# Wide experts: rows kept by chunk and gathered whole in fp32, first pair alone; a ring of eleven places with three filled during the even layer

## The chip, the cores and the metric

One NeuronCore of a Trainium2 chip runs one launch of one kernel. The metric is the device time of that launch in microseconds. Everything is fp32 in memory: 256 tokens of width 1024 go through three layers, and 578 MB are read, nearly all of it weights.

## The reference

The input `x` is [1, 256, 1024]. Three layers follow each other, each a token mixer and a mixture of experts:

```python
x = first_block(x, ...)                     # GLA + gated delta mixer, then 32 narrow experts, rms_norm
for layer in range(2):                      # second_block
    mix = even_mixer(x, ...) if layer % 2 == 0 else fourier_mixer(x, w_out)
    x = layer_norm(ALPHA * x + mix, ln1_gain[layer], ln1_bias[layer])
    ffn = hierarchical_moe_2(x, ...)        # 32 wide experts
    x = layer_norm(ALPHA * x + ffn, ln2_gain[layer], ln2_bias[layer])

# hierarchical_moe_2: every token chooses two of the 32 experts
xs = xt[tok]                                                       # rows sorted by expert
hid = silu(ragged_dot(xs, w_gate, sizes)) * ragged_dot(xs, w_up, sizes)
ys = ragged_dot(hid, w_down, sizes) * gate                         # weighted by the router
out = segment_sum(ys, tok)                                         # back to the tokens
```

The first block's experts have the hidden width 256 (narrow: 1 MB for each of the three matrices), those of the two layers of the second block 512 (wide: 2 MB each). In every layer the weights of all 32 experts are read.

## The kernel before

**Expert stage.** `stage_packed` runs once for the narrow layer (tag `one`) and once for each wide layer (tags `l0`, `l1`; the profile leaves the number out and prints `l`). It treats the experts two at a time, 16 pairs `p`, each expert with 64 slots (`CAP`), so that a pair fills 128 partitions. For each pair TensorE does, in this order:

- the gate product `hidden(p, 0, G)` (L1718): gathered rows as 64-column weights, expert weights moving, 512 columns in a wide layer, 32 records;
- two transposes of the gated one-hot matrix (L1758) into `TP`;
- the up product `hidden(p, 1, Up)` (L1718);
- `scatter(p - 1, 0)` and `scatter(p - 1, 1)` (L1728, L1729): the previous pair's output, sent back to its tokens by a product with the one-hot matrix `oneT`;
- the transposes of the hidden rows (L1770), which wait for VectorE's product of the silu and the up half (L1861);
- `scatter(p - 1, 2)` and `scatter(p - 1, 3)`. The fourth shares a PSUM bank with the first and waits for its add;
- at the end of a batch of pairs `gather(b)` (L1705, L1706): the rows of the next batch, by a product with the one-hot matrix `one`, turned on the way. Its PSUM banks are the scatter's too, so it waits for all four adds of VectorE (L1835). A batch is two pairs in a wide layer, four in the narrow one. ScalarE copies the gathered blocks out (L1796), and the next pair starts when all of a batch are out;
- `down(p)` (L1741), which waits for ScalarE's copy of the turned hidden rows (L1804).

**Split rows.** Gather and scatter multiply by a matrix of zeros and ones. To keep fp32 values whole with the `fp32r` type, each value is held as a rounded high half and the rest as a low half, and each product is done twice, once with each: `h_high` and `h_low` for the rows (ScalarE L1452, GpSimd L1477, both in the route stage), `yh` and `yl` for the pair's output (ScalarE L1814, VectorE L1871).

**Weights.** SP loads the experts' weights in chunks of 2 MB (`Experts.load`, L1618), in the order in which they are used: a wide pair has six, a narrow one three. Each chunk goes to the next place of a ring; the transfer is issued when TensorE has used up the chunk that was there before (`s_used`). A wide layer has ten places: six in `pool`, two in `gate_room`, two in `store`. The even mixer uses `pool` and `store` itself, so the first chunks of layer `l0` are issued in its route stage.

**Route stage.** `stage_out_route` does the mixer's output product (L1397), residual, normalization (L1509, L1510 write `x`), turns the rows to `hT` (L1405), computes the router's logits and picks two experts per token on VectorE (L1514 to L1563). `stage_norm` is the normalization after the experts (L1314 to L1326); it loads its gain and bias rows itself. After layer `l0` it also has SP load the Fourier tables, `w_out_fourier` and two chunks of layer `l1`; `stage_fourier` adds four, and the route stage the rest. All of SP's transfers go in the order in which SP issues them.

The stages stand behind each other with a barrier between them, in the order in `build`: mixer, route `one`, experts `one`, `stage_norm_f`, even mixer, route `l0`, experts `l0`, norm, Fourier, route `l1`, experts `l1`, norm.

## Time and profile before

| what | value |
|---|---|
| median of 3 runs | 1990.39 us (1990.31 to 1991.92) |
| the profiled execution | 1990.57 us, span 1988.7 us |
| TensorE busy | 1770.2 us, 89% of the span, mean granted clock 0.951 |
| VectorE, ScalarE, GpSimd busy | 678.9, 426.0, 83.7 us |
| read from HBM | 577.65 MB, 292 GB/s over the span |
| first wide expert stage | 984 to 1436 us |
| second wide expert stage | 1521 to 1972 us |
| a wide chunk, median from issue to landing | 28.0 to 32.6 us |

The span runs from the first to the last instruction of the profiled execution; 1.9 us of the time lie around it. In the trace a TensorE row "128\*64" is a product with 64 weight columns; two such can run at the same time, so that their mean duration is longer than their distance. A record is one instruction of the trace. The busy column of a group divided by its count is its distance when the products follow each other closely. A wait is the idle time of an engine ahead of an instruction, with the one that released it behind the arrow.

### The profile page before, as it was taken

Reading aid. Unit: us, or ns where it says so; the run is one execution under the profiler, and the core shown is the slowest. Engines: PE = TensorE matmul, PEld = TensorE weight load, DVE = VectorE, ACT = ScalarE, POOL = GpSimd, SP = SyncE. Lnnn points to the kernel's source line nnn. Section 1 sums busy time; section 2 is a strip of 40 time slices with the busy share of each in tenths; the row PEclk is TensorE's granted clock in tenths of the full one; section 3 lists DMA queues with packets and bytes.
Section 4 is the critical chain, followed back from the end, with each engine's and each line's share of the span. In section 5 each row is a group of like instructions: output and inputs, shape, how many; then the busy total and the mean of one; then the engine's idle time right before and its main releaser. Section 6 shows DMA issues by size and latency. Waiting matters only on the chain. (4 is left out here: it accounts for less than half of the span.)

```text
span 1988.7 us, 20708 instructions
## 1 busy us (share of the span) xinstructions
PE 1770.2 (89%) x8544; PEld 949.7 (48%) x8544; DVE 678.9 (34%) x1371; ACT 426.0 (21%) x705; POOL 83.7 (4%) x66
## 2 busy tenths in 40 slices
PE   7999897895789999799799999998777999998895
PEld 6884454695455555456434433333244344433331
DVE  3658242446223333543412221221333122222223
ACT  2421224452222221222211111111112111111110
POOL 0000001311100000120100000000001000000000
PEclk9999998797889999899799999999987999999998
DMA  5345230004659997341999999999795999999995
GB/s 196 128 151 176 104 122 4 0 1 188 251 237 398 403 422 283 132 170 42 408 400 423 423 423 423 424 423 423 297 382 230 424 423 423 423 423 423 423 423 225
DMA packets 100017, 581.75 MB, mean 293 GB/s; under 512 B 23947, under 2 KB 26251, under 8 KB 34893
## 3 DMA queue, kind: packets, MB, share of 16 engines
...
HBM read 577.65 MB, written 2.62 MB: 292 GB/s over the span
## 5 line engine op out<-in xcount | busy, mean ns | idle before, releaser
L1718 PE MATMUL up_ps_l<-pool,hT 128*64 128x512 f32 x640 | 143.3, 596 | 12.6 <-DMA pool<-in_expert_w_up 12.6
L1718 PE MATMUL gate_ps_l<-pool,hT 128*64 128x512 f32 x640 | 141.4, 593 | 6.6 <-DMA pool<-in_expert_w_gate 5.3
L447 PE MATMUL proj_ps<-pool,hT 128*128 128x512 f32 x320 | 141.4, 602 | 5.6 <-DVE pool L685 5.6
L1741 PE MATMUL y_ps_l<-pool,hidden_l 128*64 128x512 f32 x640 | 142.4, 596 | 2.4 <-ACT hidden_l L1804 1.4
L1871 DVE SCALAR_TENSOR_TENSOR y_low_l<-y_ps_l,slot_gate_l,y_high_l 128x512 fp32r<-128x512 f32 x64 | 47.1, 751 | 251.0 <-ACT y_high_l L1814 251.0
L439 PE MATMUL proj_ps<-hT,pool 128*128 128x256 f32 x512 | 111.9, 380 | 0.0
L1861 DVE TENSOR_TENSOR hidden_l<-hidden_l,up_ps_l 128x512 f32<-128x512 f32 x32 | 22.0, 688 | 246.8 <-PE up_ps_l L1718 246.8
L439 PEld LDWEIGHTS proj_ps<-hT,pool 128*128 128x128 f32 x512 | 96.9, 190 | 14.8 <-issue 1.8
L447 PEld LDWEIGHTS proj_ps<-pool,hT 128*128 128x128 f32 x320 | 61.8, 194 | 82.1 <-issue 75.4
L1718 PEld LDWEIGHTS gate_ps_l<-pool,hT 128*64 128x64 f32 x640 | 45.4, 137 | 98.5 <-issue 87.7
L1718 PEld LDWEIGHTS up_ps_l<-pool,hT 128*64 128x64 f32 x640 | 43.7, 137 | 98.3 <-issue 77.9
L1814 ACT ACTIVATE y_high_l<-y_ps_l,slot_gate_l 128x512 fp32r<-128x512 f32 x64 | 44.0, 688 | 203.0 <-PE y_ps_l L1741 199.5
L1741 PEld LDWEIGHTS y_ps_l<-pool,hidden_l 128*64 128x64 f32 x640 | 43.9, 137 | 88.0 <-issue 77.6
L1705 PE MATMUL gather_ps_l<-onehot_l,h_high_l 128*128 128x256 f32 x256 | 68.0, 302 | 16.9 <-DVE x L1835 12.8
L1801 ACT ACTIVATE hidden_l<-gate_ps_l 128x512 f32<-128x512 f32 x32 | 34.3, 1073 | 214.8 <-PE gate_ps_l L1718 214.8
L1804 ACT ACTIVATE hidden_l<-gate_ps_l 128x512 f32<-128x512 f32 x32 | 19.2, 599 | 278.6 <-PE gate_ps_l L1770 278.6
L1706 PE MATMUL gather_ps_l<-onehot_l,h_low_l 128*128 128x256 f32 x256 | 66.0, 295 | 0.0
L1835 DVE SCALAR_TENSOR_TENSOR x<-x,gather_ps_l 128x512 f32<-128x512 f32 x96 | 62.9, 683 | 1.6 <-PE gather_ps_l L1729 1.6
L1705 PEld LDWEIGHTS gather_ps_l<-onehot_l,h_high_l 128*128 128x128 f32 x256 | 52.0, 203 | 23.1 <-DVE x L1835 18.9
L1397 PE MATMUL out_ps_l<-store,hT 128*128 128x512 f32 x128 | 55.7, 593 | 2.4 <-PEq L2455 1.3
L1796 ACT ACTIVATE hT<-gather_ps_l 128x512 f32<-128x512 f32 x64 | 38.3, 598 | 67.0 <-PE gather_ps_l L1706 67.0
L1706 PEld LDWEIGHTS gather_ps_l<-onehot_l,h_low_l 128*128 128x128 f32 x256 | 52.2, 204 | 0.0
...
## 6 DMA issues: line engine op xcount, KB each, us to landing
...
```

The lines of the kernel that those rows point to most:

```text
L439: last = mm(pp[:, n % 2, m * T:(m + 1) * T], wbuf[n % 2][:, c, m * P:(m + 1) * P], k.hT[:, c, :], start=(c == 0), stop=(c == KC - 1))
L447: last = mm(pp[:, n % 2, j * W:(j + 1) * W], k.hT[:, c, j * P:(j + 1) * P], wbuf[n % 2][:, c, :], start=(c == 0), stop=(c == KC - 1))
L1397: last = nc.tensor.matmul(y[:, j, n, :], k.hT[:, c, j * P:(j + 1) * P], w_out[:, c, n * W:(n + 1) * W], start=(c == 0), stop=(c == KC - 1))
L1705: mm(at, k.h_high[:, j, c], moving, start=(j == 0), stop=False)
L1706: last = mm(at, k.h_low[:, j, c], moving, start=False, stop=(j == NJ - 1))
L1718: last = mm(out[e * CAP:(e + 1) * CAP, 0:H], xg(part * r + c)[:, at:at + CAP], ex.weights(i, e, c), start=(part + c == 0), stop=(part == e ...
L1741: last = mm(Y[e * CAP:(e + 1) * CAP, n], hidT[:, part * r + c, e * CAP:(e + 1) * CAP], ex.weights(i, e, c)[:, n * W:(n + 1) * W], start=(p ...
L1796: nc.scalar.activation(to, got, ACT.Copy).then_inc(s_xg, 1)
L1801: nc.scalar.activation(hid[:].rearrange("p (c n) -> p n c", c=HT), G[:, 0:H].rearrange("p (n c) -> p n c", c=HT), ACT.Silu).then_inc(s_sg, 1)
L1814: nc.scalar.activation(yh[:, n], Y[:, n], ACT.Copy, scale=slot_gate[:, 0:1]).then_inc(s_yh, 1)
L1835: nc.vector.scalar_tensor_tensor(out=xs, in0=xs, scalar=1.0 if p else alpha, in1=scatter_bank[o], op0=ALU.mult, op1=ALU.add).then_inc(s_ad ...
L1871: nc.vector.scalar_tensor_tensor(out=yl[:, n], in0=Y[:, n], scalar=slot_gate[:, 0:1], in1=yh[:, n].bitcast(F32), op0=ALU.mult, op1=ALU.sub ...
```

## The change

- The wide layers no longer split rows. The second `stt` of the normalization writes the rows by chunk into a new tile `k.h` (fp32), from which the gather and the transposes to `hT` read; ScalarE's `high` and GpSimd's subtraction stay for the narrow layer alone. The gather is one fp32 product where it was two of fp32r, and so is the scatter; `yl` and its two VectorE operations are gone there. The first pair's adds read the old rows from `k.h`.
- The batches of a wide layer are pair 0 alone, seven of two pairs, and pair 15 alone.
- Order in all three layers: the first scatter (in the last pair of a batch the first two) goes ahead of the up product, the fourth has the bank `Up` and goes behind the transposes of the hidden rows; the first two blocks of a gather go ahead of these transposes, the others behind. The gate product waits for the gathered blocks one by one.
- The ring of the wide layers has eleven places; the new one is `first_room`. Three chunks of layer `l0` are issued at the end of the even mixer's loads (`early`), six and two in its route stage; three instead of two of layer `l1` in the norm stage ahead of the Fourier mixer.
- The norm rows of `stage_norm` are loaded in the route stage (`k.ln2_rows`).
- Tiles of the even mixer and the narrow layer move into `gate_room`; `stage_norm_t` becomes `stage_turn`, with what was not used left out; the scratch that the compiler keeps in SBUF for GpSimd's transfers goes down to 1024 bytes a partition. Code that only runs when an expert has more than 64 tokens follows suit.

```diff
                     else:
                         o(stt(out=xj, in0=xj, scalar=mv[:, j, 0:1], in1=g[:], op0=ALU.subtract, op1=ALU.mult))
-                        stt(out=xj, in0=xj, scalar=rs[:, j, 0:1], in1=b_row[:],
-                            op0=ALU.mult, op1=ALU.add).then_inc(s_h, 1)
+                        by_row = "p (i c) -> p i c"
+                        stt(out=k.h[:, j].rearrange("p c i -> p i c"), in0=xj.rearrange(by_row, c=KC), scalar=rs[:, j, 0:1],
+                            in1=b_row[:].rearrange(by_row, c=KC), op0=ALU.mult, op1=ALU.add).then_inc(s_h, 1)
...
-    def __init__(self, k, before, tag, H, batch, w_gate, w_up, w_down):
-        self.tag, self.H, self.HT, self.batch, self.dram = tag, H, H // P, batch, (w_gate, w_up, w_down)
+    def __init__(self, k, before, tag, H, batch, split, w_gate, w_up, w_down):
+        self.tag, self.H, self.HT, self.split, self.dram = tag, H, H // P, split, (w_gate, w_up, w_down)
+        first = batch if split else 1
+        self.batches = [list(range(first))] + [
+            list(range(p, min(p + batch, NE // 2))) for p in range(first, NE // 2, batch)]
...
-        scatter_bank = [XG[:, 0], XG[:, 1], SC[:], XG[:, 0]]
...
-        def xg(c):
-            return xg_first[:, c] if c < here else xg_rest[:, c - here]
...
+
...
+
+            return 2 if new_batch(p) else 1
+
         def new_batch(p):
-            return p % GB == GB - 1 and p < NI - 1
+
+            b, _ = ex.batch_of[p]
+            return b + 1 if p == ex.batches[b][-1] and p < NI - 1 else 0
...
-                def gather(b):
-
-                    pe.wait_ge(s_pm, b + 1)
-                    for n in range(KC // PER):
+                def gather(b, first, end):
+
+                    width = len(ex.batches[b]) * P
+                    if first == 0:
+                        pe.wait_ge(s_pm, b + 1)
+                    for n in range(first, end):
+                        before = groups_before[b] + n
                         if n >= 2:
-                            pe.wait_ge(s_xg, b * (KC // PER) + n - 1)
-                        for m in range(PER):
-                            c = n * PER + m
-                            at = XG[:, n % 2, m * GB * P:(m + 1) * GB * P]
+                            pe.wait_ge(s_xg, before - 1)
+                        for m in range(per[b]):
+                            c = n * per[b] + m
+                            at = XG[:, n % 2, m * width:(m + 1) * width]
                             for j in range(NJ):
-                                moving = one[:, j].rearrange("p e s -> p (e s)")
-                                mm(at, k.h_high[:, j, c], moving, start=(j == 0), stop=False)
-                                last = mm(at, k.h_low[:, j, c], moving, start=False, stop=(j == NJ - 1))
+                                moving = one[:, j].rearrange("p e s -> p (e s)")[:, 0:width]
+                                if ex.split:
+                                    mm(at, k.h_high[:, j, c], moving, start=(j == 0), stop=False)
+                                    last = mm(at, k.h_low[:, j, c], moving, start=False, stop=(j == NJ - 1))
+                                else:
+                                    last = mm(at, k.h[:, j, c], moving, start=(j == 0), stop=(j == NJ - 1))
                         last.then_inc(s_gx, 1)
 
                 def hidden(p, what, out):
 
                     r = ex.rows(what)
+                    b, q = ex.batch_of[p]
                     for part in range(ex.parts):
...
                                           ex.weights(i, e, c), start=(part + c == 0),
                                           stop=(part == ex.parts - 1 and c == r - 1))
                         last.then_inc(ex.s_used, 1)
 
                 def scatter(p, o):
 
-                    if o == 3:
-                        pe.wait_ge(s_add, 4 * p + 1)
                     to_tile = oneT[:, (o // 2) * P:(o // 2 + 1) * P]
-                    mm(scatter_bank[o], to_tile, yh[:, o % 2], start=True, stop=False)
-                    mm(scatter_bank[o], to_tile, yl[:, o % 2], start=False, stop=True).then_inc(s_sc, 1)
+                    last = mm(scatter_bank[o], to_tile, yh[:, o % 2], start=True, stop=not ex.split)
+                    if ex.split:
+                        last = mm(scatter_bank[o], to_tile, yl[:, o % 2], start=False, stop=True)
+                    last.then_inc(s_sc, 1)
 
                 def down(p):
...
+                        pe.wait_ge(s_y_ready, 2 * p)
+                        pe.wait_ge(s_add, 4 * p - 4)
+                        for o in range(early(p)):
+                            scatter(p - 1, o)
                     hidden(p, 1, Up)
                     if p:
-                        pe.wait_ge(s_ys, 2 * p)
-                        if p > 1:
-                            pe.wait_ge(s_add, 4 * p - 4)
-                        scatter(p - 1, 0)
-                        scatter(p - 1, 1)
+                        for o in range(early(p), 3):
+                            scatter(p - 1, o)
+                    if b:
+                        if p:
+                            pe.wait_ge(s_add, 4 * p - 2)
+                        gather(b, 0, 2)
                     pe.wait_ge(s_hid, p + 1)
                     for m in range(HT):
                         last = nc.tensor.transpose(G[:, m * P:(m + 1) * P], hid[:, m * P:(m + 1) * P],
                                                    k.table("ident"))
                     last.then_inc(s_ht, 1)
+                    if b:
+                        gather(b, 2, groups[b])
                     if p:
-                        scatter(p - 1, 2)
                         scatter(p - 1, 3)
-                    if new_batch(p):
-                        if p:
-                            pe.wait_ge(s_add, 4 * p)
-                        gather(p // GB + 1)
                     pe.wait_ge(s_hts, p + 1)
                     down(p)
...
                     act.wait_ge(ex.s_used, gate_used(p))
                     nc.scalar.activation(hid[:].rearrange("p (c n) -> p n c", c=HT),
                                          G[:, 0:H].rearrange("p (n c) -> p n c", c=HT), ACT.Silu).then_inc(s_sg, 1)
+                    if b:
+                        gathered(b, 0, 2)
                     act.wait_ge(s_ht, p + 1)
                     nc.scalar.activation(hidT[:].rearrange("p c s -> p (c s)"), G[:, 0:HT * P],
                                          ACT.Copy).then_inc(s_hts, 1)
-                    if new_batch(p):
-                        gathered(p // GB + 1)
+                    if b:
+                        gathered(b, 2, groups[b])
                     act.wait_ge(s_slot, p + 1)
...
                                             bc(k.gates[:, :, 2 * p:2 * p + 2], 3, CAP), ALU.mult).then_inc(s_pg, 1)
 
-                def add(p):
-                    for o in range(4):
+                def add(p, first, end):
+                    for o in range(first, end):
                         dve.wait_ge(s_sc, 4 * p + o + 1)
-                        xs = k.x[:, o // 2, (o % 2) * W:(o % 2 + 1) * W]
-                        nc.vector.scalar_tensor_tensor(out=xs, in0=xs, scalar=1.0 if p else alpha, in1=scatter_bank[o],
+                        j, n = o // 2, o % 2
+                        xs, got, scale = k.x[:, j, n * W:(n + 1) * W], scatter_bank[o], 1.0 if p else alpha
+                        was = xs
+                        if p == 0 and not ex.split:
+                            by_row = "p (i c) -> p i c"
+                            xs, got = xs.rearrange(by_row, c=KC), got.rearrange(by_row, c=KC)
+                            was = k.h[:, j, :, n * (W // KC):(n + 1) * (W // KC)].rearrange("p c i -> p i c")
+                        nc.vector.scalar_tensor_tensor(out=xs, in0=was, scalar=scale, in1=got,
                                                        op0=ALU.mult, op1=ALU.add).then_inc(s_add, 1)
 
...
+                    if p:
+                        add(p - 1, 0, early(p))
                     dve.wait_ge(ex.s_used, up_used(p))
                     dve.wait_ge(s_sg, p + 1)
                     hidden = hid[:].rearrange("p (c n) -> p c n", c=HT)
                     nc.vector.tensor_tensor(hidden, hidden, Up[:, 0:H].rearrange("p (n c) -> p c n", c=HT), ALU.mult).then_inc(s_hid, 1)
                     if p:
-                        add(p - 1)
...
                         dve.wait_ge(s_add, 4 * p)
-                        dve.wait_ge(s_ys, 2 * p)
+                        dve.wait_ge(s_y_ready, 2 * p)
                     nc.vector.tensor_reduce(slot_gate[:], TP[:, 0:T], AX.X, ALU.add).then_inc(s_slot, 1)
                     nc.vector.tensor_scalar(oneT[:], TP[:, 0:T], 0.0, None, ALU.not_equal).then_inc(s_one, 1)
+                    if not ex.split:
+                        continue
                     dve.wait_ge(s_slot, p + 1)
                     for n in range(2):
                         dve.wait_ge(s_yh, 2 * p + n + 1)
                         nc.vector.scalar_tensor_tensor(
                             out=yl[:, n], in0=Y[:, n], scalar=slot_gate[:, 0:1], in1=yh[:, n].bitcast(F32),
                             op0=ALU.mult, op1=ALU.subtract).then_inc(s_ys, 1)
-                add(NI - 1)
+                add(NI - 1, 0, 4)
     k.scope = k.ctx
 
 
-def stage_general(k, tag, H, w_gate, w_up, w_down):
+def stage_general(k, ex, tag, H, w_gate, w_up, w_down):
...
                     sp.dma_start(w[n % 3][:, :, 0:width], src[:, :, a:a + width]).then_inc(s_w[n % 3], 16)
                     if name == "va":
                         load_out(k, sp, i["w_out_even"].rearrange("(p c) n -> p c n", c=KC))
+                early(sp, s["half_product"])
 
...
+            stage_turn(k, k.oa, lambda sp: ex[0].load(sp, 2))
             k.ctx = k.scope = outer
         k.retire()
+        k.gate_room = k.sb("gate_room", [P, 2 * CHUNK])
+        k.first_room = k.sb("first_room", [P, CHUNK])
+        def early(sp, s_half):
+            ex[1].load(sp, 1)
+            for products in (8, 10):
+                sp.wait_ge(s_half, products)
+                ex[1].load(sp, 1)
+
+        for region, n in ((k.first_room, 1), (k.gate_room, 1), (k.pool, 6)):
+            ex[1].ring(region, n)
+
...
+            k.norm_f_row = k.carve(k.gate_room, CHUNK, [P, D])
...
 
...
         k.dft = k.carve(k.gate_room, 0, [P, NJ, 3 * T])
-        for n in range(2):
-            ex[1 + n].ring(k.gate_room, 2)
-            ex[1 + n].ring(k.store, 2)
 
         def load_fourier(sp):
             sp.dma_start(k.dft[:], i["dft"]).then_inc(k.s_dft, 16)
             load_out(k, sp, i["w_out_fourier"].rearrange(rows_cp, p=P))
-            ex[2].load(sp, 2)
+            ex[2].load(sp, 3)
 
...
             def rest(sp, s_out):
-                ex[1 + n].load(sp, 2 if n else 8)
+                for m, row in enumerate((i["ln2_gain"], i["ln2_bias"])):
+                    sp.dma_start(k.ln2_rows[:, m], row[n:n + 1].broadcast_to([P, D])).then_inc(k.s_ln2, 16)
+                ex[1 + n].load(sp, 2 if n else 6)
                 sp.wait_ge(s_out, 4)
                 ex[1 + n].load(sp, 2)
```

## Rows read from the trace of the kernel before

**Rows 1.** Page: TensorE's granted clock and the GB/s moved, in 40 slices.

```profile
PEclk9999998797889999899799999999987999999998
...
GB/s 196 128 151 176 104 122 4 0 1 188 251 237 398 403 422 283 132 170 42 408 400 423 423 423 423 424 423 423 297 382 230 424 423 423 423 423 423 423 423 225
```

**Rows 2.** Three stretches: PE, PEld, DVE, ACT, POOL busy (x), PEclk, DMA share, GB/s.

```profile
984.29:991.72 7.43, 6.74 (x32) 6.54 (x33) 1.03 (x5) 2.42 (x5) 0.00 (x0) 0.59 1.01 427
...
991.72:1207.00 215.28, 210.15 (x1026) 85.92 (x1028) 47.13 (x80) 35.24 (x49) 0.00 (x0) 1.00 0.99 414
1207.00:1434.00 227.00, 204.11 (x960) 79.87 (x956) 49.76 (x84) 31.50 (x44) 0.00 (x0) 0.99 0.97 404
```

**Rows 3.** TensorE in order of time, second and third pair of the first wide layer: start, us.

```profile
1015.25 7.04 PE L1718 MATMUL gate_ps_l<-gate_room,hT 128*64 128x512 f32 x32
...
1033.08 0.39 PE L1705 MATMUL gather_ps_l<-onehot_l,h_high_l 128*128 128x256 f32 x1 [0.91 <-DVE x L1835]
...
1044.00 7.04 PE L1718 MATMUL gate_ps_l<-pool,hT 128*64 128x512 f32 x32
...
1058.35 0.50 PE L1728 MATMUL gather_ps_l<-y_high_l,onehot_T_l 128*128 128x512 f32 x1
...
1059.38 0.60 PE L1770 MATMUL gate_ps_l<-tables,hidden_l 128*128 128x128 f32 x4
1059.74 0.47 PE L1728 MATMUL scatter_ps_l<-y_high_l,onehot_T_l 128*128 128x512 f32 x1
...
1060.82 7.09 PE L1741 MATMUL y_ps_l<-gate_room,hidden_l 128*64 128x512 f32 x32
1067.74 7.04 PE L1718 MATMUL gate_ps_l<-store,hT 128*64 128x512 f32 x32
```

**Rows 4.** The same view, first pair, and the last pairs of both wide layers.

```profile
991.72 7.09 PE L1718 MATMUL gate_ps_l<-pool,hT 128*64 128x512 f32 x32 [0.69 <-ACT hT L1796]
...
1416.76 3.65 PE L1718 MATMUL up_ps_l<-pool,hT 128*64 128x512 f32 x16 [1.33 <-DMA pool<-in_expert_w_up]
...
1432.04 0.50 PE L1728 MATMUL gather_ps_l<-y_high_l,onehot_T_l 128*128 128x512 f32 x1 [1.58 <-DVE y_low_l L1871]
...
1528.11 7.09 PE L1718 MATMUL gate_ps_l<-pool,hT 128*64 128x512 f32 x32 [0.69 <-ACT hT L1796]
...
1968.64 0.50 PE L1728 MATMUL gather_ps_l<-y_high_l,onehot_T_l 128*128 128x512 f32 x1 [1.58 <-DVE y_low_l L1871]
```

**Rows 5.** Groups by line, shapes apart: whole fp32 products. Busy us, mean ns of one.

```profile
L439 PE MATMUL proj_ps<-hT,pool 128*128 128x256 f32 x512 | 111.9, 380 | 0.0
...
L1397 PE MATMUL out_ps_l<-store,hT 128*128 128x512 f32 x128 | 55.7, 593 | 2.4 <-PEq L2455 1.3 <-PEq L2146 1.0
...
L1172 PE MATMUL gdn_ps<-pool 128*128 128x128 f32 x192 | 25.7, 287 | 0.0
```

**Rows 6.** The first layer's router: GpSimd's and VectorE's timeline.

```profile
972.36 2.84 POOL L1477 TENSOR_TENSOR h_low_l<-x,h_high_l 128x1024 fp32r<-128x1024 f32 x1 [11.83 <-ACT h_high_l L1452]
...
973.74 1.49 DVE L1515 TENSOR_TENSOR eq_l<-logits_l,max_l 128x8 f32<-128x8 f32 x1
...
975.46 0.16 DVE L1517 TENSOR_REDUCE max_l<-eq_l 128x2 f32<-128x8 f32 x1
```

**Rows 7.** ScalarE groups: the same width written in sequence and written with a stride.

```profile
L1801 ACT ACTIVATE hidden_l<-gate_ps_l 128x512 f32<-128x512 f32 x32 | 34.3, 1073 | 214.8 <-PE gate_ps_l L1718 214.8
...
L573 ACT ACTIVATE pool<-pool 128x512 f32<-128x512 f32 x16 | 10.1, 630 | 16.4 <-DVE pool L731 16.1
```

**Rows 8.** Waits for normalization rows: VectorE's timeline, then TensorE's.

```profile
1487.94 1.28 DVE L1509 SCALAR_TENSOR_TENSOR x<-x,mean_var_l,gain_l 128x1024 f32<-128x1024 f32 x1 [2.66 <-DMA bias_l<-in_ln_bias]
...
1979.74 1.28 DVE L1324 SCALAR_TENSOR_TENSOR x<-x,mean_var_b,gain_b 128x1024 f32<-128x1024 f32 x1 [1.47 <-DMA bias_b<-in_ln_bias]
...
1490.60 1.16 PE L1405 MATMUL turned_ps_l<-tables,x 128*128 128x128 f32 x8 [1.63 <-DVE x L1510]
```

**Rows 9.** Who TensorE waited for in the narrow expert stage: us in total, times, longest.

```profile
PE gather_ps_one L1705 <- DVE x L1835: 2.9, 3, 1.0
```

221 lines of the change are left out of this document (103 added, 118 removed).

## The prediction, made before the run

> **What bounds the kernel now.** I read the page's slices first. From slice 19 on (counted from 0), the two wide expert layers (16 expert pairs each, six 2 MB chunks a pair) fill most of the run; there TensorE's granted clock stays at 0.9 or above, the 2.4 GHz level, and DMA moves 423 GB/s in slice after slice [rows 1], so a chunk takes 2.097 / 0.423 = 4.96 us and a pair 29.7 us. The stretches say which of the two is late: up to 1207 us TensorE is busy 210 of 215 us, afterwards 204 of 227 [rows 2]. TensorE starts with ten chunks in store, eats them faster than they come, and from about 1200 us waits a little ahead of most chunks (1.33 us in the row shown) [rows 4].
>
> TensorE's timeline gives its own price. A pair without a gather takes 1067.74 - 1044.00 = 23.74 us; two pairs, one with a gather, take 1067.74 - 1015.25 = 52.49, so a gather adds 5.01, of which 0.91 is a wait for VectorE [rows 3]. Sixteen pairs are 379.8; seven gathers 35.1; the first pair has no scatter (-2.1) and two bare stalls (+1.5): 414.3 us. Measured from the first gate product to the last down product: 1432.04 - 1.58 - 991.72 = 438.7 in the first layer, 1968.64 - 1.58 - 1528.11 = 438.9 in the second [rows 4]. So 24.5 us a layer is DMA wait. This is what a change can win here; it is also all the room that extra TensorE work has.
>
> **The scatter.** Now 8 single-pass fp32r products of 512 columns: 1.03 us ahead of the transposes and 1.08 behind, 2.11 a pair [rows 3]. The change makes it 4 fp32 products. The profile's fp32 products of this very shape (128x128 weights, 512 columns) are L1397: 128 records for 64 products, so two records each, 55.7 / 128 = 0.435 us a record [rows 5]. Eight records are 3.48 us. That is +1.4 a pair, and 15 scatters lie inside the layer: +20.6 us. The other end of the bound is the old rate, +0.
>
> **The gather.** Now 32 fp32r products of 256 columns, 4.1 us, and the 0.91 us wait. New: 16 fp32 products, 32 records at L439's 111.9 / 512 = 0.219 us [rows 5], 7.0 us; the wait goes, because adds 0 and 1 are done during the up product. 7.0 - 5.0 = +2.0, seven times: +14.0. The batches become 1, 2 x 7, 1, so there is an eighth gather, 128 columns wide: 32 records at L1172's 25.7 / 192 = 0.134 [rows 5], +4.3. At the old rate the seven would give -6 and the eighth +3.
>
> **Order inside a pair.** The first pair's two bare stalls (0.8 + 0.7) are covered by the new gather: -1.5. Against it, a lone scatter ahead of the up product breaks that run once more, and the copy of the turned hidden rows now hides behind one scatter instead of two. The runs of four scatter records take 1.03 and 1.08 us [rows 3], where four times 512 columns, one a cycle at 2.4 GHz, are 0.85: a switch of kinds costs 0.1 to 0.2. I take +1.5 a layer; bounds 0 and +8 (0.5 a pair).
>
> Sum between first gate and last down product: 414.3 + 20.6 + 14.0 + 4.3 - 1.5 + 1.5 = 453.2. Is DMA ever late against that? Eleven chunks are in store; the other 85 need 85 x 4.96 = 422 us from the first release, 3.5 us in, and the last must be there some 3.5 us before the end. 425 against 450: no DMA wait is left, the 24.5 us are spent and the layer is TensorE's. Per layer 453.2 - 438.8 = +14.4.
>
> **Head and tail of a wide layer.** The first gather and the wait behind it are 984.29 to 991.72, at a mean granted clock of 0.59, so mostly at the 1.2 GHz level [rows 2, 4]. 32 records of 256 columns in one pass and 16 fp32 products of 128 columns with four times the work a column are the same length at that clock; the 0.69 us wait for ScalarE's last copy goes, since waits are now by group, and the one-hot halves: -1.0. Tail: no low half of y (-0.8), but four scatters of 0.87 outrun VectorE's adds (0.68) less than now: +1.1. Together -0.7. Wide layers: 2 x 13.7 = **+27.4 us**.
>
> **Ring and early loads.** The eleventh place and the three chunks loaded in the even layer, where slices 17 and 18 move 170 and 42 GB/s [rows 1], make DMA end earlier. Worth 5 us a layer if DMA were last (one more chunk at the first release); with TensorE last, 0. The early loads stand on SP behind the last weight load of the even layer, and nothing is queued on SP behind their two waits until the block ends.
>
> **The route stages.** The high and low copies leave ScalarE and GpSimd. One of them hurt: GpSimd's subtraction runs 972.36 to 975.20, and VectorE's tiny L1515, started inside it, takes 1.49 us and ends at 975.23, where its neighbour takes 0.16 [rows 6]. That is on the path to the gather: -1.3 a layer. The page "SBUF — State Buffer" of the Trainium skill, section "Who interferes with whom", has the rule: a VectorE operation with two SBUF inputs is locked out while GpSimd reads. The trace agrees, by that 1.49.
> In exchange VectorE writes the normalized rows by chunk, 512 bytes apart. No such VectorE write is in the trace. ScalarE's are: 512 elements with such a stride 1073 ns, in sequence 630 [rows 7]. By that ratio L1510's 1.285 becomes 2.2, +0.9 a layer; bounds 0 and +1.3. The same page ("Door 1") says that consecutive accesses want to stay in one 16-byte line and pay beyond it; it speaks against this edit, and by it the price lies at the upper end. Route: -0.4 a layer, -0.8.
>
> **Rows of the norms.** Loaded ahead, they free the last stage of a 1.47 us wait [rows 8]: -1.5, all on the path. After the first wide layer a like wait goes too, but the Fourier layer's route waits for bias rows that stand in the DMA queue behind the chunks: VectorE waits 2.66 us and TensorE 1.63 behind it [rows 8]. Ahead of them the queue gets one chunk more (2.1 MB) and 1.05 MB of rows less: +1.05 / 0.423 = +2.5 us. It takes up what the norm won: **+2.5**, bounds 0 and +5.
>
> **Narrow layer.** Its arithmetic and batches stay; gathers lose their wait, 2.9 us in all [rows 9], the first 0.7; the pairs get the same two breaks, 15 x 0.25 = +3.8. Net 0, bounds -3 and +5.
>
> **Sum.** 27.4 - 0.8 - 1.5 + 2.5 + 0 = +27.6 us. The profiled execution took 1990.57 us (span 1988.7 and 1.9 around it), 0.2 above the median of 1990.39, so one serves for the other. 1990.6 + 27.6 = **2018 us**.
>
> **Rivals.**
> 1. DMA stays last (faster). If the whole fp32 products ran at the fp32r rate, TensorE's sum would be about 410 and the layer would end with DMA: one chunk sooner, 5 us, and 0.8 of tail, twice, and 0.2 of the rest: 1990.6 - 11.4 = 1979. It decides wherever the layer's TensorE sum stays under some 433, that is if the 39 us added above were under 19. Against it: three groups of rows with two records a product [rows 5]. The page "FP8 and Floating Point Precision" (Trainium skill, "TensorE Precision Notes") counts four passes for true fp32, which is the rows' reading and not this rival's. Chance 0.05.
> 2. The added order costs more: 0.5 us at each of three places of every pair, because ScalarE and VectorE answer later than the short covers. 15 x 1.5 less the 1.5 counted, twice, and the narrow layer's 5: +47, 2065; a milder half of it 2040. For it: the transposes-to-down stretch has lost a scatter. Against it: in the wide layer a single scatter (0.87) is about what two were (1.08). Chance 0.09.
> 3. DMA waits stay on top of the new TensorE work: the ring refills in bursts of release and the 24.5 us remain. 2018 + 49 = 2067. Against it: eleven chunks are nearly two pairs, and the sum above leaves 25 us. Chance 0.03.
> 4. The change does nothing measurable because the extra work fits exactly into the wait: 1986 to 1995. It needs +24 where I count +39. Chance 0.03.
>
> **How the numbers follow.** Forecast 2018, chance 0.80; its own range is 2008 to 2029 from the bounds of order, stride, queue and narrow layer. The range reaches a little into the milder half of rival 2 and no further: 2006 to 2032. A measurement of this kernel can tell about 0.2% (4 us) from no change. Faster 0.06 (rival 1 and part of 4), same 0.02, slower 0.92.
>
> **What would show it.** Right: no waits of L1718 and L1741 for DMA in the wide layers after the first pairs; SP waiting for TensorE and GB/s below 423 there; scatter records at 0.435, gather records at 0.219; 453 us between first gate and last down product; L1515 back at 0.17. Wrong: waits for DMA late in the layer and a pair without a gather near 24 us (rival 1); gaps of half a microsecond around the transposes (rival 2). What would make the prediction wrong is above all the fp32 rate in this order of products, short runs of four between 64-column ones.

## The result and the profile after

The changed kernel takes 2016.18 us (median of 4 runs, 2015.4 to 2016.61); the kernel before took 1991.16 us beside it (4 runs, 1990.31 to 1992.39). The ratio is 1.0125, 95% interval 1.0107 to 1.0142: slower by 1.25%, clear of 1. The forecast was 2018 us, with 2006 to 2032. The profiled span is 2013.6 us, 24.9 above the 1988.7 of before.

The page's clock and GB/s slices come first (beside [rows 1]), then four stretches of the first wide layer (beside [rows 2]): PE, PEld, DVE, ACT, POOL busy (x), PEclk, DMA share, GB/s.

```profile
PEclk9999998897899999899799999999897999999998
...
GB/s 193 126 155 183 106 103 4 1 1 237 197 298 412 413 413 188 250 172 191 334 406 424 424 424 424 423 424 425 135 377 261 407 424 424 424 424 424 424 424 57
```

```profile
978.20:984.53 6.33, 6.33 (x32) 6.21 (x32) 1.03 (x5) 0.60 (x1) 0.00 (x0) 0.57 0.16 66
984.53:1207.00 222.47, 222.47 (x981) 90.60 (x982) 37.86 (x64) 33.94 (x48) 0.00 (x0) 1.00 0.98 410
1207.00:1400.00 193.00, 193.00 (x848) 76.68 (x844) 31.65 (x55) 27.51 (x39) 0.00 (x0) 1.00 1.01 424
1400.00:1439.00 39.00, 38.72 (x185) 15.54 (x182) 7.00 (x12) 5.63 (x9) 0.00 (x0) 1.00 0.34 142
```

TensorE is busy for all of the 193 us from 1207 to 1400; before, it stood still for 23 of the 227 us behind 1207. DMA still moves 424 GB/s in the middle, but the last slice has fallen from 225 to 57 and the layer's own last 39 us to 142: the chunks have landed before TensorE is through.

TensorE in order of time, a pair with a gather (beside [rows 3]):

```profile
1038.74 3.60 PE L1718 MATMUL gate_ps_l<-gate_room,hT 128*64 128x512 f32 x16
...
1045.71 0.44 PE L1757 MATMUL turn_ps_l<-tables,gated_onehot_l 128*128 128x128 f32 x2
1045.98 1.88 PE L1726 MATMUL gather_ps_l<-y_high_l,onehot_T_l 128*128 128x512 f32 x4
1047.80 7.09 PE L1718 MATMUL up_ps_l<-pool,hT 128*64 128x512 f32 x32
1054.82 1.13 PE L1726 MATMUL scatter_ps_l<-y_high_l,onehot_T_l 128*128 128x512 f32 x2
1055.78 3.62 PE L1703 MATMUL gather_ps_l<-onehot_l,rows_by_chunk 128*128 128x256 f32 x16
1059.23 0.60 PE L1775 MATMUL gate_ps_l<-tables,hidden_l 128*128 128x128 f32 x4
1059.67 3.62 PE L1703 MATMUL gather_ps_l<-onehot_l,rows_by_chunk 128*128 128x256 f32 x16
1063.12 1.02 PE L1726 MATMUL up_ps_l<-y_high_l,onehot_T_l 128*128 128x512 f32 x2
1064.08 7.09 PE L1741 MATMUL y_ps_l<-pool,hidden_l 128*64 128x512 f32 x32
1070.99 3.60 PE L1718 MATMUL gate_ps_l<-pool,hT 128*64 128x512 f32 x16
```

No row has a wait. By the starts, the gather takes (1059.23 - 1055.78) + (1063.12 - 1059.67) = 6.90 us, the scatter 1.82 + 0.96 + 0.96 = 3.74, the whole pair 32.25 us. The body, from the first gate product to the end of the last down product, is 1438.72 - 984.53 = 454.19 us in the first wide layer and 1993.02 - 1538.83 = 454.19 in the second; it was 438.7 and 438.9 [rows 4].

Where the 24.9 us of span came from, stage by stage, each from the start of a TensorE run to the start of another in both traces ("last scatter" is the start of the last pair's first scatter):

| stretch | before | after | difference |
|---|---|---|---|
| start to the narrow layer's first gather | 552.93 | 552.99 | +0.1 |
| narrow layer, first gather to last scatter | 250.09 | 246.49 | -3.6 |
| from there to the even layer, and the even layer | 130.24 | 128.63 | -1.6 |
| route of the first wide layer | 51.03 | 50.09 | -0.9 |
| first wide layer, first gather to last scatter | 447.75 | 461.31 | +13.6 |
| last scatter to the Fourier layer's dft | 18.48 | 18.51 | 0.0 |
| dft to the second wide layer's gather | 70.55 | 75.70 | +5.2 |
| second wide layer, first gather to last scatter | 447.57 | 460.09 | +12.5 |
| last scatter to the end | 20.06 | 19.79 | -0.3 |

### The profile page after: what moved, and what is told of

The parts are those of the page before. It is cut to its first block and busy times, and to the rows that moved or that the text cites. A ratio compares the mean times of both kernels' runs of the same rounds, so it can differ in the third digit from the quotient of the medians.

```text
span 2013.6 us, 20759 instructions
## 1 busy us (share of the span) xinstructions
PE 1856.1 (92%) x8608; PEld 985.4 (49%) x8608; DVE 641.6 (32%) x1309; ACT 415.7 (21%) x701; POOL 72.2 (4%) x62
## 5 line engine op out<-in xcount | busy, mean ns | idle before, releaser
L1741 PE MATMUL y_ps_l<-pool,hidden_l 128*64 128x512 f32 x576 | 128.1, 595 | 0.0
L1718 PE MATMUL up_ps_l<-pool,hT 128*64 128x512 f32 x576 | 127.9, 595 | 0.0
L1718 PE MATMUL gate_ps_l<-pool,hT 128*64 128x512 f32 x576 | 127.3, 592 | 0.0
L1703 PE MATMUL gather_ps_l<-onehot_l,rows_by_chunk 128*128 128x256 f32 (+1 forms) x576 | 120.6, 366 | 3.5 <-DVE onehot_l L1827 3.5
L1703 PEld LDWEIGHTS gather_ps_l<-onehot_l,rows_by_chunk 128*128 128x128 f32 x576 | 102.5, 200 | 22.2 <-issue 8.3
L1818 ACT ACTIVATE y_high_l<-y_ps_l,slot_gate_l 128x512 f32<-128x512 f32 x64 | 44.0, 687 | 209.5 <-PE y_ps_l L1741 206.0
L1832 DVE TENSOR_TENSOR gated_onehot_l<-onehot_l,gates 128x256 f32<-128x256 f32 x32 | 13.6, 425 | 194.8 <-PE turn_ps_l L1757 194.2
L1803 ACT ACTIVATE hidden_l<-gate_ps_l 128x512 f32<-128x512 f32 x32 | 34.1, 1067 | 195.6 <-PE gate_ps_l L1718 195.6
L1726 PE MATMUL gather_ps_l<-y_high_l,onehot_T_l 128*128 128x512 f32 x128 | 64.7, 608 | 1.6 <-ACT y_high_l L1818 1.6
L1845 DVE SCALAR_TENSOR_TENSOR x<-x,gather_ps_l 128x512 f32<-128x512 f32 x60 | 40.8, 686 | 53.2 <-PE gather_ps_l L1726 53.2
L1845 DVE SCALAR_TENSOR_TENSOR x<-x,up_ps_l 128x512 f32<-128x512 f32 x30 | 20.6, 687 | 107.4 <-PE up_ps_l L1726 107.4
```

Source lines behind the costliest of these rows:

```text
L1703: last = mm(at, k.h[:, j, c], moving, start=(j == 0), stop=(j == NJ - 1))
L1718: last = mm(out[e * CAP:(e + 1) * CAP, 0:H], xg(part * r + c)[:, 0, at:at + CAP], ex.weights(i, e, c), start=(part + c == 0), stop=(part = ...
L1726: last = mm(scatter_bank[o], to_tile, yh[:, o % 2], start=True, stop=not ex.split)
L1741: last = mm(Y[e * CAP:(e + 1) * CAP, n], hidT[:, part * r + c, e * CAP:(e + 1) * CAP], ex.weights(i, e, c)[:, n * W:(n + 1) * W], start=(p ...
L1803: nc.scalar.activation(hid[:].rearrange("p (c n) -> p n c", c=HT), G[:, 0:H].rearrange("p (n c) -> p n c", c=HT), ACT.Silu).then_inc(s_sg, 1)
L1818: nc.scalar.activation(yh[:, n], Y[:, n], ACT.Copy, scale=slot_gate[:, 0:1]).then_inc(s_yh, 1)
```

## The experiments

All are edits of the changed kernel, of which the main lines are shown, and all ratios are to the kernel before, run beside them on the same chip. The median of that kernel moved from one group of runs to the next (1991.2, 1992.7, 1994.1, 1994.7 us), so the ratios and the stretches of the trace are compared, not bare times; the start of the narrow layer moved by up to 8.6 us from trace to trace ahead of the wide layers, which these edits are about.

### Which arithmetic costs what: four kernels

A ring of eleven leaves no room for the low parts, so three split kernels have ten places, and a fourth with ten places and nothing else stands beside them. In all four, three chunks instead of four are issued during the Fourier layer.

Scatter split:

```diff
-        yh = k.sb(f"y_high_{tag}", [P, 2, W], DT)
-        yl = k.sb(f"y_low_{tag}", [P, 2, W], DT) if ex.split else None
+        yh = k.sb(f"y_high_{tag}", [P, 2, W], F32R)
+        yl = k.sb(f"y_low_{tag}", [P, 2, W], F32R)
...
-                    last = mm(scatter_bank[o], to_tile, yh[:, o % 2], start=True, stop=not ex.split)
-                    if ex.split:
+                    last = mm(scatter_bank[o], to_tile, yh[:, o % 2], start=True, stop=False)
+                    if True:
                         last = mm(scatter_bank[o], to_tile, yl[:, o % 2], start=False, stop=True)
```

> The changed kernel, but the scatter of the two wide layers goes back to two fp32r products (high and low part of y), and the ring has ten places, which is all that fits beside the low part (six instead of seven chunks of the last layer are issued ahead of its routing). Theory (TensorE ends last, the four-pass products are the loss): the scatter costs 20.6 us less in each wide layer, so the body falls from 454.2 to about 433.6 us if no chunk is waited for. At that length the DMAs are about as long as TensorE, so some of it comes back as waits for chunks: 1975 to 1986 us, likeliest 1980. Rival (the order, not the arithmetic, made the body longer): 2005 us or more.

Gather split:

```diff
-                        by_row = "p (i c) -> p i c"
-                        stt(out=k.h[:, j].rearrange("p c i -> p i c"), in0=xj.rearrange(by_row, c=KC), scalar=rs[:, j, 0:1],
-                            in1=b_row[:].rearrange(by_row, c=KC), op0=ALU.mult, op1=ALU.add).then_inc(s_h, 1)
+                        stt(out=xj, in0=xj, scalar=rs[:, j, 0:1], in1=b_row[:],
+                            op0=ALU.mult, op1=ALU.add).then_inc(s_h, 1)
...
-                                if ex.split:
+                                if True:
                                     mm(at, k.h_high[:, j, c], moving, start=(j == 0), stop=False)
                                     last = mm(at, k.h_low[:, j, c], moving, start=False, stop=(j == NJ - 1))
```

> The changed kernel with a ring of ten, but the rows of the two wide layers are gathered as high and low fp32r parts again, made by ScalarE and GpSimd as before; the scatter stays whole. Theory: the gathers cost 14 to 18 us less in each wide layer, body 454.2 to about 438, TensorE still last or nearly: 1986 us (1981 to 1992). Rival (order): 2005 us or more.

Both edits together:

> The changed kernel with a ring of ten and both the gather and the scatter of the wide layers split into fp32r products again: only the new order, the first pair alone, the early chunks and the norm rows are left of the change. Theory: TensorE's own work falls to about 416 to 418 us a layer, the DMAs end last at 434 to 439 us, with 15 to 20 us of waits for chunks back in each wide layer: 1983 us (1976 to 1990), hardly below the kernel with the split scatter alone, because both rest on the DMAs. Rival (TensorE goes on being last, each saving adds up): 2016 - 2 x 36 = 1944 us.

The ring alone:

```diff
-RING = 11
+RING = 10
...
-                stage_fourier(k, lambda sp: ex[2].load(sp, 4))
+                stage_fourier(k, lambda sp: ex[2].load(sp, 3))
...
-                ex[1 + n].load(sp, 2 if n else 6)
+                ex[1 + n].load(sp, 2 if n else 5)
```

> The changed kernel with a ring of ten instead of eleven places, and six instead of seven chunks of the last layer ahead of its routing; nothing else. Theory: with TensorE last the eleventh place is worth nothing: 2016 us, within 2 us. Rival (the eleventh place keeps the chunks ahead of TensorE, its loss brings waits of up to 5 us a layer): 2026 us.

Measured: scatter split 1985.49 us, ratio 0.9956 (0.9937 to 0.9974); gather split 1987.89, 0.9977 (0.9964 to 0.9990); both 1986.15, 0.9974 (0.9959 to 0.9989); ring of ten alone 2012.86, 1.0104 (1.0074 to 1.0133). The body of the first wide layer, one row for each kernel, in the order after, scatter split, gather split, both split (same columns as above; every row has 2009 matmul records):

```profile
984.53:1438.72 454.19, 454.19 (x2009) 182.81 (x2008) 76.52 (x131) 66.85 (x95) 0.00 (x0) 1.00 0.94 393
```

```profile
986.44:1427.22 440.78, 432.52 (x2009) 182.25 (x2008) 96.83 (x161) 67.31 (x95) 0.00 (x0) 1.00 0.98 410
```

```profile
993.88:1435.20 441.32, 436.02 (x2009) 167.64 (x2008) 75.16 (x131) 66.90 (x95) 0.00 (x0) 0.99 0.98 409
```

```profile
986.35:1427.18 440.83, 416.68 (x2009) 166.08 (x2008) 95.45 (x161) 67.30 (x95) 0.00 (x0) 0.99 0.98 410
```

Read two columns against each other. By TensorE's busy time the whole gather adds 432.52 - 416.68 = 15.8 us (18.2 where the scatter is whole too), the whole scatter 436.02 - 416.68 = 19.3 (21.7). The length doesn't follow it: undoing one product, the other, or both all end at 441 us. With both split TensorE stands still for 24.2 us, and the list of its waits in that stretch (us in total, times, longest; its first rows) says for what:

```profile
PE up_ps_l L1716 <- DMA pool<-in_expert_w_up: 9.1, 7, 1.6
PE gate_ps_l L1716 <- DMA pool<-in_expert_w_gate: 5.6, 5, 1.3
PE y_ps_l L1739 <- ACT hidden_l L1806: 2.0, 9, 0.2
```

All its rows with a DMA add up to 22 us. So 441 us is the DMA end with ten places, and 454.2 is TensorE's.

The busy column isn't clean as a price: it gives two values for each product. The two kernels with a split gather start their body at the low clock (the granted clock is 0.50 up to 990 us in the one with both split), which lengthens their first pair. The pairs that wait for no chunk are cleaner. Here are the starts of three pairs with both products split:

```profile
1014.37 7.04 PE L1716 MATMUL gate_ps_l<-pool,hT 128*64 128x512 f32 x32
...
1038.43 7.04 PE L1716 MATMUL gate_ps_l<-pool,hT 128*64 128x512 f32 x32
...
1066.01 7.04 PE L1716 MATMUL gate_ps_l<-store,hT 128*64 128x512 f32 x32
```

| a pair, us | before | after | scatter split | gather split | both split |
|---|---|---|---|---|---|
| without a gather | 23.74 | 25.34 | 24.06 | 25.34 | 24.06 |
| with a gather | 28.75 | 32.25 | 30.67 | 29.17 | 27.58 |

The whole gather costs 3.1 us each time, seven times 21.7. The whole scatter costs 1.3 us, and 1.6 in a pair with a gather: 21.3 over fifteen. (The 24.06 hold a wait of 0.2 us for ScalarE's copy, which the whole scatter covers.) The eighth gather, for one pair, costs the same in both forms. Split, its 32 records of 128 columns take 1391.38 - 1387.85 = 3.53 us; whole, they take 1404.90 - 1401.33 = 3.57:

```profile
1387.85 0.22 PE L1698 MATMUL gather_ps_l<-onehot_l,h_high 128*128 128x128 f32 x1
...
1391.38 0.63 PE L1773 MATMUL gate_ps_l<-tables,hidden_l 128*128 128x128 f32 x4
```

So TensorE's work with both split is, as an estimate from these pairs, 454.2 - 21.7 - 21.3 = 411 us. The rival that the order made the body longer (2005 us or more) is out: the new order with split products stands at 0.9974 of before, not above it. The ring of ten alone leaves the body at 454.19 in both layers: with TensorE last the eleventh place is worth nothing. That kernel was nevertheless lower than the changed one by two thousandths, which I hadn't expected (the intervals overlap). In the trace its difference lies between the dft and the next gather (75.7 before the edit, 68.8 us with it), which led to the next experiment.

### The chunks ahead of the bias rows

```diff
-                stage_fourier(k, lambda sp: ex[2].load(sp, 4))
+                stage_fourier(k, lambda sp: ex[2].load(sp, 2))
...
-                ex[1 + n].load(sp, 2 if n else 6)
+                ex[1 + n].load(sp, 4 if n else 6)
```

> The changed kernel, but during the Fourier layer SP issues two chunks of the last layer's weights instead of four ahead of the last layer's gain and bias rows, and four instead of two behind them. Theory: the 6.3 us that VectorE waited for the bias rows at 1498.8 us, and the fall of TensorE's clock after the wait of 6.0 us that it caused, both go; from the first Fourier product to the last layer's gather 75.7 falls to 68.5 us, the bodies stay at 454.2: 2016 - 7 = 2009 us. Rival (those chunks are missed later, as waits in the last layer): 2016 us or more, with waits for chunks in its first pairs.

Measured: 2012.39 us, 1.0087 (1.0068 to 1.0107); against the 1.0125 of the changed kernel that is -0.4%, 7 to 8 us. From the dft to the gather it is 67.7 instead of 75.7 us, and the bodies stay at 454.2. The changed kernel's VectorE and TensorE at this place (beside [rows 8]):

```profile
1498.80 1.28 DVE L1472 SCALAR_TENSOR_TENSOR x<-x,mean_var_l,gain_l 128x1024 f32<-128x1024 f32 x1 [6.32 <-DMA bias_l<-in_ln_bias]
```

```profile
1479.70 16.47 PE L1357 MATMUL out_ps_l<-store,hT 128*128 128x512 f32 x38
1502.14 1.97 PE L1365 MATMUL turned_ps_l<-tables,rows_by_chunk 128*128 128x128 f32 x8 [5.97 <-DVE rows_by_chunk L1474]
1503.90 8.00 PE L1357 MATMUL out_ps_l<-store,hT 128*128 128x512 f32 x16
```

and with two chunks ahead:

```profile
1504.73 1.04 PE L1365 MATMUL turned_ps_l<-tables,rows_by_chunk 128*128 128x128 f32 x8
1505.60 7.03 PE L1357 MATMUL out_ps_l<-store,hT 128*128 128x512 f32 x16
```

The wait is 5.97 us, and behind it the same 8 transposes take 1.97 instead of 1.04 and the same 16 records 8.00 instead of 7.03. The granted clock in the changed kernel's stretches (columns as above) is the reason:

```profile
1496.17:1502.14 5.97, 0.00 (x1) 0.00 (x1) 3.31 (x3) 0.00 (x0) 0.00 (x0) 0.74 0.46 89
1502.14:1506.50 4.36, 4.36 (x12) 2.94 (x13) 1.16 (x2) 1.19 (x2) 0.00 (x0) 0.57 0.88 365
1506.50:1511.70 5.20, 5.20 (x13) 2.28 (x12) 0.00 (x0) 0.00 (x0) 0.00 (x0) 1.00 1.01 424
```

During the idle 5.97 us the grant falls from the 2.4 GHz to the 1.2 GHz level and is back only after some 4 us of work. The wait cost itself and 0.93 + 0.97 = 1.9 us more than with two chunks ahead. Before, a 1.63 us wait at this place [rows 8] was followed by 7.03 us for the 16 records; only the transposes were slightly longer (1.16). The theory holds; the two late chunks aren't missed.

### The order: first pair alone or not

```diff
-        first = batch if split else 1
+        first = batch
```

> The changed kernel, but the first gather of a wide layer takes two pairs as before, so there are eight gathers of two pairs and no gather for a single pair. Theory: in the body seven gathers of 7.0 us stay and the last one, for one pair (about 4.8 us), goes: 454.2 to about 449.4 us in each wide layer; the first gather runs while the clock is still low and grows from 6.3 us to between 9.3 us (6.3 x 7.0/4.8) and 14: +3 to +7.7. Sum: -4 to +6 us over both layers, likeliest 2017 us. Rival (the first pair alone saves its time because the first products start sooner and chunks come free sooner): 2022 us or more.

Measured: 2023.34 us, 1.0140 (1.0122 to 1.0158), +3 us against the changed kernel; the intervals overlap, but the stretches show it. The body is 452.18 instead of 454.19, and the first gather is longer:

```profile
984.73 9.69 PE L1703 MATMUL gather_ps_l<-onehot_l,rows_by_chunk 128*128 128x256 f32 x32 [2.01 <-DVE onehot_l L1827]
994.35 3.65 PE L1718 MATMUL gate_ps_l<-first_room,hT 128*64 128x512 f32 x16
...
1009.62 0.66 PE L1775 MATMUL gate_ps_l<-tables,hidden_l 128*128 128x128 f32 x4 [0.79 <-DVE hidden_l L1873]
1010.96 7.09 PE L1741 MATMUL y_ps_l<-pool,hidden_l 128*64 128x512 f32 x32 [0.69 <-ACT hidden_l L1808]
```

9.62 us to the first gate product against 6.33, +3.3 (+3.9 in the second layer). The last gather (3.6 us at full clock) goes from the body, but the two bare stalls of the first pair, 0.8 and 0.7, are back: -2.0. Sum +1.3 and +1.9. The first gather begins at the low clock in both kernels (mean grant 0.57 over the 6.33 us, 0.73 over the 9.62), so with the first pair alone less of the gathering is done there and more at the full clock: it is worth about 3 us over both layers. The bare 2023.34 us lies where I had put the rival (2022 us or more, a mechanism with chunks that come free sooner) and above my range, but the kernel before, run beside it, was 3 us higher too (1994.1); 1.0140 of its 1991.16 us is 2019, inside the range. And the rival has nothing for it in the rows: neither kernel waits for a chunk.

### The rows by chunk

```diff
-                        by_row = "p (i c) -> p i c"
-                        stt(out=k.h[:, j].rearrange("p c i -> p i c"), in0=xj.rearrange(by_row, c=KC), scalar=rs[:, j, 0:1],
-                            in1=b_row[:].rearrange(by_row, c=KC), op0=ALU.mult, op1=ALU.add).then_inc(s_h, 1)
+                        stt(out=k.h[:, j], in0=xj, scalar=rs[:, j, 0:1], in1=b_row[:],
+                            op0=ALU.mult, op1=ALU.add).then_inc(s_h, 1)
...
-                                    last = mm(at, k.h[:, j, c], moving, start=(j == 0), stop=(j == NJ - 1))
+                                    last = mm(at, k.h[:, j, c:D:KC], moving, start=(j == 0), stop=(j == NJ - 1))
```

> The changed kernel, but the norm leaves the rows in row order in the new tile, and the transposes, the gathers and the first addition of a wide layer read them with the stride of 32 bytes there. Theory: the write of 1024 columns falls from 1.98 to about 1.29 us, twice in each wide layer, and TensorE's weight loads don't feel the stride: -1.4 to -2.8 us, 2013 to 2015 us. Rival (a strided weight load is slower and shows beside the gather's matmuls): 32 loads in each of nine gathers at 0.05 us or more give +15 us a layer, 2045 us.

(The transposes and the first addition read the tile in the same way.) Measured: 2037.93 us, 1.0222 (1.0207 to 1.0236), 19 us above the changed kernel: my theory was wrong and the rival's mechanism right, at 10 us a layer where it had 15. Here is the weight load of the gather between 1055 and 1067 us (busy us, mean ns), changed kernel first, rows in row order second:

```profile
L1703 PEld LDWEIGHTS gather_ps_l<-onehot_l,rows_by_chunk 128*128 128x128 f32 x32 | 6.0, 190 | 1.2 <-issue 0.5
```

```profile
L1702 PEld LDWEIGHTS gather_ps_l<-onehot_l,rows_by_chunk 128*128 128x128 f32 x32 | 7.9, 335 | 0.4 <-issue 0.2
```

and what it does to a gather of one pair at the end of the first wide layer, in the same order:

```profile
1401.33 3.73 PE L1703 MATMUL gather_ps_l<-onehot_l,rows_by_chunk 128*128 128x128 f32 x32
```

```profile
1408.36 7.65 PE L1702 MATMUL gather_ps_l<-onehot_l,rows_by_chunk 128*128 128x128 f32 x32
```

A weight load with steps of 32 bytes takes 335 ns instead of 190. Behind 256 moving columns most of it hides (6.90 to 7.74 us for the two halves, by their starts); behind 128 columns nothing does, and the gather takes twice as long. Seven times 0.84 and once 3.9 are 9.8 us; the bodies are 464.1 instead of 454.2, and the first gathers, ahead of them, 7.8 us instead of 6.3 and 5.1. On VectorE the write indeed fell from 1.96 to 1.28 us (first row: changed kernel; second: this one), and the first wide layer's route with it by 0.6 us, the second's by 1.4:

```profile
961.21 1.96 DVE L1474 SCALAR_TENSOR_TENSOR rows_by_chunk<-x,rstd_l,bias_l 128x1024 f32<-128x1024 f32 x1
```

```profile
961.40 1.28 DVE L1473 SCALAR_TENSOR_TENSOR rows_by_chunk<-x,rstd_l,bias_l 128x1024 f32<-128x1024 f32 x1
```

### A version that beats both, and the early chunks

The balance is that TensorE needs 454 us with everything whole and some 433 with the scatter split, and that the DMAs need 441 with ten places. Whole gathers, a split scatter and eleven places bring both ends near 435. The room for the low part of y comes from the second norm's rows, which go into a ring place once its last chunk is used; the Fourier layer gets three chunks.

```diff
-        k.ln2_rows = k.sb("ln2_rows", [P, 2, D])
+        k.ln2_rows = k.carve(k.gate_room, CHUNK, [P, 2, D])
...
-                stage_fourier(k, lambda sp: ex[2].load(sp, 4))
+                stage_fourier(k, lambda sp: ex[2].load(sp, 3))
...
-                ex[1 + n].load(sp, 2 if n else 6)
+                ex[1 + n].load(sp, 3 if n else 6)
...
+            def rows_last(sp):
+                e = ex[1 + n]
+                last = max(c for c in range(e.total) if c % e.room == 8)
+                sp.wait_ge(k.s_chunk_used, e.used0 + last + 1)
+                for m, row in enumerate((i["ln2_gain"], i["ln2_bias"])):
+                    sp.dma_start(k.ln2_rows[:, m], row[n:n + 1].broadcast_to([P, D])).then_inc(k.s_ln2, 16)
```

> Meant as the best version: the changed kernel with whole gathers, but the scatter split into two fp32r products; the ring keeps eleven places because the second norm's rows are loaded late into a used place and free 8 KB for the low part of y; three chunks of the last layer during the Fourier layer instead of four. Theory: TensorE's own work is 434 to 435 us a layer, the DMAs need one chunk of 4.95 us less than with ten places (440.8 - 4.95 = 435.9), so the body is 436 to 438 us: about 4 us a layer below the kernel with the split scatter and ten places, 0.991 of the kernel before, 1973 us (1970 to 1978). Rival (the eleventh place is worth nothing, because the DMAs stand idle before the layer for another reason): body 440.8, 1981 us.

Measured: 1973.22 us, 0.9892 (0.9876 to 0.9908), against 0.9956 with ten places: the bodies are 435.40 and 435.19. Against the split scatter with ten places (440.8 and 441.0) the eleventh place is worth 5.4 and 5.8 us, a little more than the 4.96 us of one chunk; in the changed kernel it was worth 0. Little is left for a twelfth, which wasn't tried: TensorE is busy for 431.6 of the 435.4 us, and waits for chunks for 1.6 of them in the first layer. Two more kernels, the changed one and this one, each without the three chunks in the even layer:

```diff
-            ex[1].load(sp, 1)
-            for products in (8, 10):
-                sp.wait_ge(s_half, products)
-                ex[1].load(sp, 1)
+            return
...
-                ex[1 + n].load(sp, 2 if n else 6)
+                ex[1 + n].load(sp, 2 if n else 9)
```

> The changed kernel without the three chunks issued during the even layer; they are issued with the others after the first wide layer's rows. Theory (TensorE last): the ring fills by about 983 + 15 = 998 us instead of 979, TensorE takes the first chunks from 984.5 on and the last ones not before 1010, so nothing waits: body 454.2, 1.0125 of the kernel before, 2016 us within 2 us. Rival (the early chunks carry the start of the layer): first waits for chunks, up to 15 us.

> The best version (split scatter, whole gather, eleven places) without the three chunks issued during the even layer. Theory: there the DMAs and TensorE end nearly together. The ring was full 10.5 us before its first place came free; three chunks are 14.9 us, so the DMAs are behind by 4.4 us more in the first wide layer and nothing in the second: body 435.4 to 437 to 440 in the first, 435.2 in the second, 0.9892 to 0.990 to 0.9915 of the kernel before, 1977 us. Rival (nothing waits there either): 435.4 in both.

(The three chunks are issued with the six others behind the first wide layer's rows.) Measured: 2017.37 us, 1.0125 (1.0101 to 1.0150), and 1972.90 us, 0.9891 (0.9873 to 0.9910), where I had 1977. In the changed kernel the early chunks do nothing: both bodies stay at 454.2. In the best version the DMAs work through where they had stood still. With the early chunks, then without:

```profile
985.00:990.00 5.00, 5.00 (x30) 5.00 (x31) 1.03 (x5) 0.60 (x1) 0.00 (x0) 0.65 0.00 2
990.00:995.00 5.00, 5.00 (x27) 1.93 (x27) 0.00 (x0) 1.88 (x2) 0.00 (x0) 1.00 0.01 3
```

```profile
985.00:990.00 5.00, 5.00 (x34) 3.45 (x34) 0.00 (x0) 2.48 (x3) 0.00 (x0) 0.91 1.01 429
990.00:995.00 5.00, 5.00 (x26) 1.62 (x22) 0.00 (x0) 0.07 (x1) 0.00 (x0) 1.00 1.02 423
```

and its first body grows by 1.6 us (435.40 to 436.99), where I had 1.6 to 4.6, while the second stays (435.06). The ratio can't tell 1.6 us; I take it from the trace alone.

## Why the prediction was right

**What bounds it.** Right: the layer waited for chunks, and the kernel with both products split shows it again: TensorE busy 416.7 of 440.8 us. The 24.5 us are what the length had above the sum of the pairs; the idle time that the trace before puts down to chunks in the first wide layer is 18.5 us (TensorE busy 412.3 of 438.7).

**The scatter.** Right. The estimate from L1397's record was 3.48 us a pair; its three runs in the pair above take 3.74, with the breaks. I had +20.6 us a layer; by the pairs with and without the split it is 21.3, of which 2.1 are the 0.3 more in pairs with a gather.

**The gather.** Right: it adds 32.25 - 25.34 = 6.91 us to its pair where it added 5.01, +13.3 for seven against +14.0. This +1.9 is the 3.1 of the whole form, the 0.3 of the scatter beside it, and -1.5 for the wait of 0.91 and what the new order saves beyond it. Its records are 0.216 us from start to start where L439 gave 0.219, so a product of 256 columns takes 0.43 us against 0.12 for a single fp32r pass. That is what the four passes of the Trainium skill's page "FP8 and Floating Point Precision" ("TensorE Precision Notes") make of it. By the rows of this case the ratio is 3.6. The eighth was sized a little high, 3.6 instead of 4.3 us, and the split form would have needed as much.

The same two forms from 984 to 1993 us of the trace after (beside [rows 5]; busy us, mean ns):

```profile
L1703 PE MATMUL gather_ps_l<-onehot_l,rows_by_chunk 128*128 128x256 f32 x448 | 101.5, 380 | 0.0
...
L1726 PE MATMUL gather_ps_l<-y_high_l,onehot_T_l 128*128 128x512 f32 x124 | 62.7, 607 | 0.8 <-ACT y_high_l L1818 0.8
```

**The order in a pair.** Taken too cheap: the new order alone, with both products split, makes a pair 24.06 us where it was 23.74 (0.2 of it the wait for ScalarE's copy), +4.8 over fifteen, against the +1.5 that I took (bounds 0 and 8). It hardly shows because other terms are smaller than forecast: the scatter without the order is 15 x 1.28 = 19.2 (-1.4), the gathers -0.7, the eighth -0.7. Together +0.5 of the 1.0 us by which the body, 454.19, is above my 453.2; the rest isn't assigned. The first pair's two stalls are covered, as forecast (-1.5). Rival 2 (2065) is out: TensorE has no wait in the body.

**Ring and early loads.** Right: 0 for both with TensorE last. The 5 us a layer that I gave the ring for the case of DMA last were 5.4 and 5.8 in the best version.

**Route.** The lock went: L1479 (L1515 before, 1.49 [rows 6]) takes 0.17. It is GpSimd's work that made it: in the kernel with the split gather, where GpSimd subtracts again, the operation takes 1.49 once more and ends with the subtraction. First the changed kernel, then that one:

```profile
969.25 0.17 DVE L1479 TENSOR_TENSOR eq_l<-logits_l,max_l 128x8 f32<-128x8 f32 x1
```

```profile
975.21 2.84 POOL L1439 TENSOR_TENSOR h_low<-x,h_high 128x1024 fp32r<-128x1024 f32 x1 [11.83 <-ACT h_high L1414]
976.59 1.49 DVE L1477 TENSOR_TENSOR eq_l<-logits_l,max_l 128x8 f32<-128x8 f32 x1
```

This is what the Trainium skill's page "SBUF — State Buffer" ("Who interferes with whom") says of a VectorE operation with two SBUF inputs beside a GpSimd one that reads SBUF, and here the experiment shows it. The strided write took 1.96 to 2.00 us where 2.2 was expected from ScalarE's ratio: the price (+0.7) was a little smaller. The same page of the Trainium skill ("Door 1") says that there is a price and not how large; that it would be the upper end (2.6) was my reading, and too much. Route of the first layer -0.9 instead of -0.4: -1.3 and +0.7, and the one-hot matrix, now 0.42 instead of 0.69, which I had counted in the head of the expert stage.

**Norm rows and the queue.** Right in mechanism and size, with one cost left out. From SP's first issue behind the first wide layer to VectorE's start with the bias rows it is 1498.80 - 1445.42 = 53.4 us, and it was 1487.94 - 1436.64 = 51.3: +2.1 where I had +2.5. VectorE itself came there 1.6 us sooner, since the norm had its rows, so its wait grew from 2.66 to 6.32, and this is the part that takes up what the norm won. TensorE's wait grew by 4.3, from 1.63 to 5.97, because the first of the two strided writes (+0.7) also stands on the path here. Then the clock fell: +1.7 by the starts, 0.76 on the transposes and 0.97 on the records behind them. What I left out was that a longer wait doesn't only move the work behind it but makes it slower. The router's 0.6 and 0.3 in the Fourier products come off, which gives the +5.2 of the table. At the end the norm starts without its wait (-1.5), and the longer tail of adds, which I had at +1.1 (measured +1.2), takes most of it back: -0.3.

**Narrow layer.** Wrong by 3.6 us. I had put 15 x 0.25 = +3.8 for the breaks against the waits that go; pairs without a gather cost +0.08 (13.28 to 13.36), not +0.25, and each of the three gathers saved 1.25. The term of the breaks was taken too large: +1.2 for fifteen, which is 2.6 of the 3.6; most of the rest is that a gather saved more than its wait of 1.0.

**Even layer.** Not in the sum: -1.6 us. Its first 32 half products take 15.4 instead of 17.0 us; the clock rose earlier there (mean grant 0.90 over them, 0.82 before). Why it did wasn't tried and stays open.

The stretches of the table against the forecast for the same stretches, with the tail of +1.1 put behind each wide layer, where it lies:

| stretch | forecast | measured |
|---|---|---|
| both wide layers, first gather to last scatter | +25.2 | +26.1 |
| behind the first one, to the next gather | +3.2 | +5.2 |
| last scatter to the end | -0.4 | -0.3 |
| route of the first wide layer | -0.4 | -0.9 |
| narrow layer | 0 | -3.6 |
| even layer | 0 | -1.6 |

The errors are +0.9, +2.0, +0.1, -0.5, -3.6 and -1.6. The first three (+3.0) take back half of the last three (-5.7), and the sum was 2.7 us too high against the span. A hit of 2 us in the whole is therefore partly luck: the two wide layers were right to 4%, but with the order's error against those of the other terms, and the small stretches were not right. The range had a slip as well: its own bounds add up to 2008 at the lower end, but at the upper end to 2018 + 13 + 0.8 + 2.5 + 5 = 2039, not to the 2029 that I wrote.

**The rivals.** The first (DMA stays last) needed a TensorE sum under some 433 us. The experiments show that the place was about right: with TensorE busy for 432.5 us and ten places the body is 440.8, DMA's end, and with eleven 435.4. The change stands at 454. The third had no trace in the rows. Of the second a fifth came: 0.3 us a pair of the 1.5 that it needs, and none of it as a wait in the changed kernel. The fourth (an exact fit) needed +24 on my 414.3 and got +39.9.
